# Bidirectional gated linear attention, heads 1 to 3: decay differences and exponentials issued in the head ahead, query products ahead of key products

## The reference, cut to what matters

```
qs = qc * jnp.exp(b - b_mid)
ks = kc * jnp.exp(b_mid - b)
s = jnp.where(mask, jnp.einsum('bihk,bjhk->bhij', qs, ks), 0.0)
o = jnp.einsum('bhij,bjhv->bihv', s, vc)
o = o + jnp.einsum('bihk,bhkv->bihv', qc * jnp.exp(b), state)
kd = kc * jnp.exp(b_last[:, None] - b)
state = state * jnp.exp(b_last)[..., None] + jnp.einsum('bjhk,bjhv->bhkv', kd, vc)
```

## Time and profile before

| | us |
|---|---|
| median of 3 runs | 2164.12 |
| lowest and highest | 2163.28, 2167.95 |
| the profiled execution's own time | 2166.34 |
| its span in the trace | 2164.6 |
| PE busy | 1992.0 (92%) |
| DVE busy | 1607.6 (74%) |
| ACT busy | 1225.3 (57%) |
| the four GLA heads | from about 98 to 317 of the span |

### The profile page before, as it was taken

How to read it: one execution, slowest core, us unless ns; L and a number is a source line. 1 busy time by engine, 2 the same in 40 slices (tenths; PEclk the granted TensorE clock), 3 DMA queues, 4 the chain that set the end, 5 groups by cost and what they waited for, 6 DMA issues and landing times. The chain is left out here.

```text
span 2164.6 us, 26048 instructions
## 1 busy us (share of the span) xinstructions
PE 1992.0 (92%) x9242; PEld 1610.8 (74%) x9242; DVE 1607.6 (74%) x1544; ACT 1225.3 (57%) x1057; POOL 245.8 (11%) x172
## 2 busy tenths in 40 slices
PE   6898987999978999859999999999999999999992
PEld 4777766677766888737888888888888888888882
DVE  4654538778665226358999999999999999999993
ACT  5444434446343213226777777777777777777763
POOL 0000004542612000001000000000000001010100
PEclk9999898999989999859999999999999999999996
DMA  5222234532524934438999999999999999999982
GB/s 133 66 78 68 69 90 157 162 128 87 171 81 155 312 118 144 160 127 318 354 374 363 375 363 371 359 374 365 373 362 373 362 372 363 373 361 372 365 311 85
DMA packets 212049, 541.08 MB, mean 250 GB/s; under 512 B 16438, under 2 KB 131544, under 8 KB 175064
## 3 DMA queue, kind: packets, MB, share of 16 engines
q1 hardware_dynamic: 204600, 518.54, 66.0%
q0 software_dynamic: 7392, 21.77, 4.3%
HBM read 512.87 MB, written 31.59 MB: 252 GB/s over the span
## 5 line engine op out<-in xcount | busy, mean ns | idle before, releaser
L1951 DVE TENSOR_TENSOR w_low<-ring_a,w_high 128x2048 fp32r<-128x2048 f32 x192 | 435.4, 2286 | 42.2 <-ACT w_high L1945 41.8
L1951 DVE TENSOR_TENSOR w_low<-ring_b,w_high 128x2048 fp32r<-128x2048 f32 x192 | 435.7, 2286 | 40.8 <-ACT w_high L1945 40.5
L1945 ACT ACTIVATE w_high<-ring_b 128x2048 fp32r<-128x2048 f32 x192 | 368.2, 1919 | 155.6 <-PE ps L2045 109.3
L1945 ACT ACTIVATE w_high<-ring_a 128x2048 fp32r<-128x2048 f32 x192 | 367.9, 1918 | 151.9 <-PE ps L2045 109.6
L2045 PE MATMUL ps<-w_high,rows_high 128*128 128x512 f32 x1024 | 403.7, 394 | 1.3 <-DVE w_low L1951 1.3
L2045 PE MATMUL ps<-w_high,rows_low 128*128 128x512 f32 x1024 | 400.3, 391 | 0.0
L2045 PE MATMUL ps<-w_low,rows_high 128*128 128x512 f32 x1024 | 399.5, 390 | 0.0
L2045 PEld LDWEIGHTS ps<-w_high,rows_high 128*128 128x128 f32 x1024 | 193.0, 188 | 44.1 <-DVE w_low L1951 4.6
L2045 PEld LDWEIGHTS ps<-w_high,rows_low 128*128 128x128 f32 x1024 | 192.6, 188 | 41.1
L2045 PEld LDWEIGHTS ps<-w_low,rows_high 128*128 128x128 f32 x1024 | 193.1, 189 | 39.6
L2109 PE MATMUL ps<-w_high,act_high 128*128 128x512 f32 x512 | 207.0, 404 | 15.2 <-DVE w_low L1951 7.6
(11 more groups left out here) (344 smaller groups left out, 2935.1 us busy)
## 6 DMA issues: line engine op xcount, KB each, us to landing
ring_a<-in_w SPq DMA_DIRECT2D x192, 1024.0 KB, 7.8
ring_b<-in_w SPq DMA_DIRECT2D x192, 1024.0 KB, 7.9
unit_raw<-in_w_in SPq DMA_DIRECT2D x80, 512.0 KB, 4.3
temps<-cum_rows SPq DMA_DIRECT2D x16, 1024.0 KB, 7.5
unit_raw<-in_w_up_ssd SPq DMA_DIRECT2D x16, 512.0 KB, 4.6
ssd_out_T<-y_high SPq DMA_DIRECT2D x4, 1024.0 KB, 6.3
ssd_out_T<-y_low SPq DMA_DIRECT2D x4, 1024.0 KB, 6.7
ssd_high<-ssd_out_T SPq DMA_DIRECT2D x4, 1024.0 KB, 11.7
```

Of the source, the lines that this page charges most:

```text
L1945: nc.scalar.activation(w_hi[:, split_at(it, j)], slot(at, 1)[:, 0, :], ACT.Copy).then_inc(w_hi_ok, 1)
L1951: nc.vector.tensor_tensor(w_lo[:, split_at(it, j)], slot(at, 1)[:, 0, :], w_hi[:, split_at(it, j)].bitcast(F32), ALU.subtract).then_inc(w_ ...
```

## The change: what it does

`gla_diffs` is the part of `gla_dve` that writes the differences. For heads 1 to 3 DVE now runs it in the head ahead, behind the state updates and ahead of the low halves called "after" and of the normalisation; it waits for `o_ps` of that head, as before. ACT runs the next head's exponentials of direction 0 between `o_ps` and the squares, and those of direction 1 between the square root and the "end" pieces. The products are regrouped: the two `dec` copies, then the six products with q, then the six with k, and only then the low halves of "d0" and "d1". PE's only new number is the wait of the KD transposes: all six q products and the KD product of that direction.

```diff
--- before.py
+++ after.py
@@ -444,7 +444,7 @@
                 piece(pe, n)
 
             def transposes(d):
-                pe.wait_ge(g_qk, h * 12 + 6 * d + 1)
+                pe.wait_ge(g_qk, h * 12 + 3 * d + 7)
                 if d:
                     pe.wait_ge(kd_ok, h * 2 + 1)
                 elif h:
@@ -515,9 +515,9 @@
 
         def gla_act(act, h):
             at_step = HEAD_PIECES[h]
-            gla_exps(act, h, 0)
-            gla_exps(act, h, 1)
             if h == 0:
+                gla_exps(act, h, 0)
+                gla_exps(act, h, 1)
                 takes(act, (6, 7))
             takes(act, at_step["start"])
 
@@ -533,6 +533,8 @@
             takes(act, at_step[0])
             takes(act, at_step[1])
             act.wait_ge(o_ps, h + 1)
+            if h + 1 < HEADS:
+                gla_exps(act, h + 1, 0)
             for t in range(NT):
                 if t or h:
                     act.wait_ge(o_sq, h * 5 + t)
@@ -540,6 +542,8 @@
                                      accum_out=stat[:, 16 + t:17 + t]).then_inc(o_sq, 1)
             act.wait_ge(o_v, h * 6 + 1)
             nc.scalar.activation(stat[:, 24:28], stat[:, 20:24], ACT.Sqrt).then_inc(o_sq, 1)
+            if h + 1 < HEADS:
+                gla_exps(act, h + 1, 1)
             takes(act, [n for n in at_step["end"] if n < N_GROUP[0] + 9])
             if h == HEADS - 1:
                 piece_take(act, N_GROUP[0] + 9)
@@ -555,8 +559,7 @@
                        {"d0": (22,), "d1": (23,), "scan": (24, 25), "loop": (), "after": (26,), "o": (27,)},
                        {"d0": (), "d1": (), "scan": (28,), "loop": (29,), "after": (30, 31), "o": (32, 33)})
 
-        def gla_dve(v, h):
-            splits = HEAD_SPLITS[h]
+        def gla_diffs(v, h):
             for d in range(2):
                 at_b = h * SEQ + d * HEADS * SEQ
                 b = cumg[:, at_b:at_b + SEQ]
@@ -570,22 +573,32 @@
                 off, b4 = by_half(g_e[d][OFF]), by_half(b)
                 nc.vector.tensor_tensor(off[:, :, d, :], edge, b4[:, :, d, :], ALU.subtract).then_inc(g_diff, 1)
                 nc.vector.tensor_tensor(off[:, :, 1 - d, :], b4[:, :, 1 - d, :], edge, ALU.subtract).then_inc(g_diff, 1)
-            v.wait_ge(pc_taken, N_HEAD[h] + 2)
+
+        def gla_dve(v, h):
+            splits = HEAD_SPLITS[h]
+            if h == 0:
+                gla_diffs(v, h)
+            q, k = qk_w[h % 2]
             for d in range(2):
-                v.wait_ge(g_exp, h * 10 + 5 * d + 2)
+                v.wait_ge(g_exp, h * 10 + 5 * d + 1)
                 if h:
                     v.wait_ge(st_ok, h * 6)
                 nc.vector.tensor_copy(dec[:, d, :].unsqueeze(2), by_tile(g_e[d][QI])[:, :, LAST[d]:LAST[d] + 1]).then_inc(g_dec, 1)
-                q, k = qk_w[h % 2]
-                nc.vector.tensor_tensor(g_e[d][KD], g_e[d][KD], k, ALU.mult).then_inc(g_qk, 1)
+            v.wait_ge(pc_taken, N_HEAD[h] + 1)
+            for d in range(2):
+                v.wait_ge(g_exp, h * 10 + 5 * d + 5)
                 v.wait_ge(g_dec, h * 2 + d + 1)
                 nc.vector.tensor_tensor(g_e[d][QI], g_e[d][QI], q, ALU.mult).then_inc(g_qk, 1)
-                v.wait_ge(g_exp, h * 10 + 5 * d + 5)
-                nc.vector.tensor_tensor(g_e[d][KS], g_e[d][KS], k, ALU.mult).then_inc(g_qk, 1)
                 nc.vector.tensor_tensor(g_e[d][QS], g_e[d][QS], q, ALU.mult).then_inc(g_qk, 1)
                 off = by_half(g_e[d][OFF])
+                nc.vector.tensor_tensor(off[:, :, 1 - d, :], off[:, :, 1 - d, :], by_half(q)[:, :, 1 - d, :], ALU.mult).then_inc(g_qk, 1)
+            v.wait_ge(pc_taken, N_HEAD[h] + 2)
+            for d in range(2):
+                nc.vector.tensor_tensor(g_e[d][KD], g_e[d][KD], k, ALU.mult).then_inc(g_qk, 1)
+                nc.vector.tensor_tensor(g_e[d][KS], g_e[d][KS], k, ALU.mult).then_inc(g_qk, 1)
+                off = by_half(g_e[d][OFF])
                 nc.vector.tensor_tensor(off[:, :, d, :], off[:, :, d, :], by_half(k)[:, :, d, :], ALU.mult).then_inc(g_qk, 1)
-                nc.vector.tensor_tensor(off[:, :, 1 - d, :], off[:, :, 1 - d, :], by_half(q)[:, :, 1 - d, :], ALU.mult).then_inc(g_qk, 1)
+            for d in range(2):
                 for n in splits[f"d{d}"]:
                     split_low(v, n)
             v.wait_ge(s_ps, h + 1)
@@ -617,6 +630,8 @@
                 if s == 1:
                     for n in splits["loop"]:
                         split_low(v, n)
+            if h + 1 < HEADS:
+                gla_diffs(v, h + 1)
             for n in splits["after"]:
                 split_low(v, n)
             if h == 0:
```

## The result

| | before | changed |
|---|---|---|
| median, us | 2166.03 (4 runs, 2163.28 to 2169.97) | 2185.26 (4 runs, 2182.55 to 2188.95) |
| profiled execution, us | 2166.34 | 2182.55 |
| its span, us | 2164.6 | 2180.8 |
| ratio | | 1.0089, 95% interval 1.0062 to 1.0115 |

The changed kernel is slower by 19.2 us by the medians (the 0.0089 with its interval is 13 to 25 us), by 16.2 in the two profiled executions (two of the four runs, the profiled one among them, are near 2182.6, two near 2188.4; what sets them apart was not traced). The forecast was 2181.7, 17.6 more than the median it was made from.

A forecast was written before the change was run, and what follows sets the result against it. No engine alone bounds it: PE stops where the transfer, high half and low half ring or a head's chain is late. 4.0 + 5.4 + 7.7 + 0.5 = 17.6 on 2166.34 gives 2183.9, median 2.2 lower: 2181.7; range 2172 to 2188.

The forecast's parts named there:

- The end of head 0: Head 0 to head 1's scores: squares 4.24 us late, 3.75 saved on differences, 7.74 paid; +4.0 us.
- the sum: Three head ends plus clock loss: 4.0 + 5.4 + 7.7 + 0.5 = 17.6 us, no absorption expected behind them.
- lower bound: Whole kernel: 2175.0 us, if one table load does not hold (1.3), clock losses go (4.4) and landings are quicker (1.0).
- The end of head 1: Head 1 to L479 of head 2: late low halves delay unit 21, then exponentials, squares and unit 25; +5.4 us.
- The end of head 2: Head 2 to quad 24: high half and low half 27 come 7.74 us late, nothing given back; +7.7 us.
- (b): Behind the heads, such as head 3's transfer waits: slack swallows most of the shifts, 2160 to 2168 us; chance 0.05.
- The regrouping alone costs nothing: Products of each head: the twelve take 6.30 us in any order and the scores wait for all; cost zero.
- the first paragraph: Stretch with four heads: TensorE waits 15.7 us for low halves and 9.3 for products, ACT 38.2 for raw weights.
- (a): Head ends: the old head's tail is covered, only the products' chain counts; 9 to 12.5 us gained; chance 0.04.
- (c): Head ends: only two of the three terms hold, as when unit 21 does not gate exponentials; 2170 to 2175; 0.11.
- (d): Three places: idle times of 4 and 5 us, each followed by long 1.2 GHz stretches; 2187 to 2191 us; 0.10.

The follow-up runs named there:

- e1: Kernel before, with differences and exponentials issued early for head 1 alone, products in the old order: 1.0013 against before.
- e5: Changed kernel with DVE writing the low halves called "after" ahead of the differences: 1.0076 against the kernel before.
- e3: Kernel before, with differences and exponentials issued early for head 3 alone, products in the old order: 1.0026 against before.
- e4: Changed kernel with only the product regrouping and PE's wait kept, differences and exponentials where they were before: 1.0039 against before.
- e9: Changed kernel with the old product order and PE's old wait, differences and exponentials still early in all three heads: 1.0080 against before.
- e2: Kernel before, with differences and exponentials issued early for head 2 alone, products in the old order: 1.0012 against before.
- e7: Kernel before, with differences and some exponentials of heads 1 and 2 moved only into existing engine waits: 0.9967 against before, median 2157.69 us.

## Why the prediction was right

**The end of head 0** (+4.0): 25.3 us instead of 21.1 to the scores, +4.2; squares 4.2 late (4.24 worked out), PE idle until the transposes 4.24. Right step by step, and e1 gives it alone. What the sum had not subtracted is that less low clock lies behind the scores' shorter wait: from o0 to o1 it is 2.9. The prediction had this loss (1.0) in its lower bound only.

**The end of head 1** (+5.4): L479 shifted by 6.4. The chain went as written (from o1: piece 18 at 5.1, high half 21 at 9.0 and squares at 14.2, for which 5.0, 9.0 and 14.1 were worked out; piece 20 at 23.9 for 23.7). The last steps were too short in the prediction: unit 25 landed 5.6 us after low half 22 began instead of 5.2, and the KD transposes took 1.1 instead of 0.6, at a granted clock of 0.50. e5 shows 4.0 of it to come from the low halves behind the differences.

**The end of head 2** (+7.7 and 0.5 of clock): quad 24 at 16.1 for 8.4, and 1.1 us of clock: the two pieces took 13.9 instead of 12.8. e3 gives it alone, and its profile shows that the slack of head 3 swallows none, which was rival (b). From o2 to the first piece behind the heads it is 9.6 in all, where the prediction had 8.2.

**"The regrouping alone costs nothing"** was the step that failed: e4 puts it at 6.8 us on its own (5 to 12 timed), and e9 at up to 3.6 inside the change, of which 1.2 at L479 is clear. Three things were missed there. The sum had part of it under another name, the late low half 22 in the term of head 1. Where exponentials are not early, q first means waiting for the last of them before a single k product is done. And the KD transposes, which were called harmless because the scores wait for all twelve products anyway, moved into PE's wait, with the low clock behind it.

**What was luck.** In the stage the profile has 18.3 for a sum of 17.6. By heads it has 2.9, 5.9 and 9.6 (with rounding), and the prediction 4.0, 5.4 and 8.2: the first too large, the others too small, and part of the fit is that these cancel. The chain of waits is what held up.

**Two readings beside the sum.** Of the 15.7 us that PE waits for low halves, 10.5 are the one wait behind the heads, so it stops less inside them than the first paragraph says. And the change adds six table loads at the three ends, not five (at 129.06, 136.76, 196.58, 204.15, 243.64 and 251.35 us of the changed kernel); the steps of the sum have all six.

**Rivals.** (a) is refuted by e1: the tail of the old head is not covered, and head 1's chain pays for it more than it gains. (c) does not hold, since all three shifts are there. (d) asked for 5 us or more of low clock. Pieces 18 and 19 did take 13.85 us instead of 11.18, and 20 and 21 12.76 instead of 11.15, but behind each pair PE waited again before the next link of the chain (0.70 us for DVE, 2.69 for ACT); the 1.1 at quad 24 is what was left on the path. The size of 17.6 lies inside the measured interval of 13 to 25.

## What to carry to other kernels

In these runs, work moved ahead of a wait helped only where its engine idled at the new place. Before moving it, look at what stands behind the new place on the same engine: here an eight-instruction block in front of two small low halves held a transfer, and that transfer held the other engine. Two engines' parts of one step can be moved separately, and the table of idle times says where; the part put into such waits gained 7.7 us in this stage by the profiles, the same kind of work put in front of the normalisation, with the regrouping, lost 18.

## What the runs showed of the hardware

The same instruction after the same idle time ran at either clock. L479 of head 0, in the profile of before and then of the changed kernel, the order of work ahead of it on PE being equal; the granted clock over it was 0.54 in the first and 1.00 in the second:

```profile
116.05 3.64 PE L479 MATMUL ps<-temps 128*128 128x256 f32 x8 [1.90 <-DVE temps L602]
...
115.55 2.00 PE L479 MATMUL ps<-temps 128*128 128x256 f32 x8 [1.90 <-DVE temps L615]
```

With the 0.5 us that the two were apart before it, this puts o0 at 131.12 in one and 128.98 in the other; over the ten experiments it lies at 128.3 to 132.4. So 2 us between two single profiles are no evidence here, and it is why the table counts from o0. Two pieces show the same: behind an idle time of 1.75 to 1.77 us they took 12.79 us before, at a granted clock of 0.87, and 11.18 in e2 and e7, at 1.00. Table loads took 1.28 us each, and where nothing else held it the next function began 1.29 to 1.30 after the load had begun, in the timelines read here: no time for a drain shows.
